# A two-block transformer forward on one core: finer places for the steps of the hybrid layers, and new orders for three engines

## The reference

```python
# first block, each of 2 layers (D_FF 2816)
f = swiglu(rms_norm(h, g1), w_gate, w_up, w_down);  h = h + 0.5 * rms_norm(f, g1_post)
u = rms_norm(h, mix_pre_g);  parts = split(u @ w_in)
y_a = short conv (3 taps);  y_b = conv (31 taps) + layer norm + silu
y_c = differential attention (4 heads);  y_d = forgetting attention (8 heads)
merged = sum(sigmoid(gate_i) * (y_i @ w_out_i));  h = h + rms_norm(merged @ w_o, mix_post_g)
f = swiglu(rms_norm(h, g2), ...);  h = h + 0.5 * rms_norm(f, g2_post)
# second block, each of 2 hybrid layers
z = rms_norm(h, g_norm) @ w_in              # 2656 columns
oa = dense GQA (q, k normed, axial rope);  ob = windowed GQA with a sink (rope)
oc = latent attention: q from a rank 192 part of z, k and v from a rank 128 part
h = h + concat(oa, ob, oc) * silu(gates) @ w_out
# at the end
return rms_norm(h, final_g)
```

## Time and profile before

| | us |
|---|---|
| median of 3 runs | 1691.02 |
| lowest, highest | 1689.95, 1692.52 |
| profiled execution, its own time | 1691.12 |
| span in its profile, first to last instruction | 1689.3 |
| TensorE busy in the span | 1646.0 |
| VectorE, ScalarE busy | 1098.7, 815.8 |

### The profile page before, as it was taken

The page is one execution under the profiler, slowest core; times in us unless marked ns, Lnnn a source line. Parts: engine busy times, 40 slices in busy tenths (PEclk is TensorE's granted clock), DMA queues, the critical chain, the costliest instruction groups (busy, mean ns, idle before and its releaser), DMA issues.

```text
span 1689.3 us, 21552 instructions
## 1 busy us (share of the span) xinstructions
PE 1646.0 (97%) x8719; PEld 1395.1 (83%) x8719; DVE 1098.7 (65%) x1314; ACT 815.8 (48%) x1116; POOL 36.5 (2%) x60
## 2 busy tenths in 40 slices
PE   8999999999999999999999999999999998999997
PEld 7888799978887888788888998788888887778776
DVE  6444668898666454655456799975665455766665
ACT  5443544454445443454445454544544446664653
POOL 0000000000000000000000000000000000000000
PEclk9999999999999999999999999999999999999999
DMA  8555465444556555565546545355555545224421
GB/s 311 196 179 199 165 219 178 162 175 150 175 174 218 181 195 182 179 216 181 194 155 224 189 168 193 126 174 195 192 206 193 181 150 162 100 93 141 135 75 50
DMA packets 67427, 292.70 MB, mean 173 GB/s; under 512 B 7152, under 2 KB 11648, under 8 KB 51456
## 3 DMA queue, kind: packets, MB, share of 16 engines
q1 hardware_dynamic: 63984, 279.47, 48.2%
q10 hardware_dynamic: 3344, 11.85, 2.0%
HBM read 290.23 MB, written 1.06 MB: 172 GB/s over the span
## 4 chain that ended last, share of the span: by engine, by line
PE 82%; DVE 9%; issue 3%; ACT 3%; DVEq 2%; DMA 1%; POOL 0%; ACTq 0%; POOLq 0%; SPq 0%
PE ps L1573 24%; PE ps L1575 24%; PE ps L1574 24%; DVE wlo L1046 3%; PE ps L2045 2%; PE ps L1736 1%; DVE mix L1243 1%; DVEq L1248 1%; PE ps L2071 1%; PE ps L1671 1%; ACT tmp L699 1%; PE ps L2056 1%; PE ps L1708 1%; PE ps L1641 1%; DVE small L1335 1%
## 5 line engine op out<-in xcount | busy, mean ns | idle before, releaser
L1046 DVE TENSOR_TENSOR wlo<-raw,whi 128x2048 fp32r<-128x2048 f32 (+2 forms) x269 | 601.2, 2243 | 259.4 <-ACT whi L696 253.9
L696 ACT ACTIVATE whi<-raw 128x2048 fp32r<-128x2048 f32 (+2 forms) x269 | 500.3, 1872 | 130.7 <-DMA raw<-stream 129.4
L1573 PE MATMUL ps<-whi,xhi 128*128 128x512 f32 (+1 forms) x1024 | 404.1, 395 | 1.1 <-ACT mix L960 1.1
L1575 PE MATMUL ps<-whi,xlo 128*128 128x512 f32 (+1 forms) x1024 | 396.2, 387 | 0.0
L1574 PE MATMUL ps<-wlo,xhi 128*128 128x512 f32 (+1 forms) x1024 | 396.2, 387 | 0.0
L1573 PE MATMUL ps<-whi,yar 128*128 128x512 f32 x620 | 245.5, 396 | 2.0 <-DVE yar L1560 1.5
L1574 PE MATMUL ps<-wlo,yar 128*128 128x512 f32 x620 | 241.0, 389 | 0.0
L1575 PE MATMUL ps<-whi,yar 128*128 128x512 f32 x620 | 241.0, 389 | 0.0
L1573 PEld LDWEIGHTS ps<-whi,xhi 128*128 128x128 f32 x1024 | 192.8, 188 | 40.7 <-issue 4.5
L1575 PEld LDWEIGHTS ps<-whi,xlo 128*128 128x128 f32 x1024 | 192.7, 188 | 39.0
L1574 PEld LDWEIGHTS ps<-wlo,xhi 128*128 128x128 f32 x1024 | 192.9, 188 | 35.3
(11 more groups left out here) (217 smaller groups left out, 1361.6 us busy)
## 6 DMA issues: line engine op xcount, KB each, us to landing
raw<-stream SPq DMA_DIRECT2D x262, 512.0 KB, 4.7
raw<-stream SPq DMA_DIRECT2D x122, 1024.0 KB, 4.8
raw<-stream SPq DMA_DIRECT2D x22, 384.0 KB, 3.9
gpre<-pre_gain ACTq DMA_DIRECT2D x8, 512.0 KB, 4.2
gpost<-post_gain ACTq DMA_DIRECT2D x6, 512.0 KB, 5.3
mix<-cum ACTq DMA_DIRECT2D x2, 1024.0 KB, 6.8
raw<-stream SPq DMA_DIRECT2D x6, 256.0 KB, 6.8
raw<-stream SPq DMA_DIRECT2D x4, 320.0 KB, 4.4
```

What stands on the lines that cost most here:

```text
L696: A(whi[:, s, 0:w], raw[:, s, 0:w], ACT.Copy).then_inc(hi_ready, 1)
L1046: TT(wlo[:, s, 0:w], raw[:, s, 0:w], whi[:, s, 0:w].bitcast(F32), ALU.subtract).then_inc(lo_v, 1)
L1573: pe.matmul(dst, lh, rh, start=first, stop=False)
L1575: return pe.matmul(dst, ll, rh, start=False, stop=last)
```

## The change

No instruction is added to or removed from the matmuls, activations or vector operations, and no tile changes its size. Four things change.

1. In the hybrid layers a half of a chunk no longer is one step but four (one k tile of a wide chunk with its 3 matmuls, two k tiles of a gate with their 6), so a chunk has eight places between which other steps of TensorE can stand. Each token half of an `out` chunk's first pass has two. Chunks of the mixing stage have two.
2. The hybrid layers' tables of all three engines have new numbers throughout.
3. In the mixing stage TensorE's `scores` 5 goes ahead of `turn` 4. On VectorE two steps of the convolution go a step earlier, the split for chunk 29 (`split` 26) goes from ahead of `scores` 5 to behind `values` 4, and `out` 2 goes behind `split` 31, `weigh` 7 and `values` 6.
4. In `boundary`, in the six that end an FFN or a mixing stage, VectorE's `low` for t = 0, second half, stands behind the two updates of `h` of t = 1, where it stood ahead of them.

The waits keep their semaphores and values; where a step became several, the wait stands at its first part. The diff, cut:

```diff
-    at(pe, (19.02, 21.02, 23.02, 25.04, 27.02, 29.02, 31.02, 33.02), "turn")
+    at(pe, (19.02, 21.02, 23.02, 25.04, 27.1998, 29.02, 31.02, 33.02), "turn")
...
     for p in range(AT_WOUT):
-        for half in range(2):
-            pe.append((p + half / 2 + 0.4, "chunk", p, half))
+        for part in range(8):
+            pe.append((p + (0.4, 0.425, 0.45, 0.475, 0.9, 0.925, 0.95, 0.975)[part], "chunk", p, part // 4, part % 4))
     for n in range(4):
-        pe.append((AT_WOUT + n / 2 + 0.4, "out", n))
-    at(pe, (3.52,), "l_turn")
-    at(pe, (6.02, 6.2376, 6.54, 6.56, 9.02, 9.04, 10.52, 10.54), "flip")
+        for part in range(2):
+            pe.append((AT_WOUT + n / 2 + 0.4 + part / 20, "out", n, part))
+    at(pe, (3.1197,), "l_turn")
+    at(pe, (5.4052, 6.1126, 6.4028, 6.4617, 8.9693, 9.1434, 10.4986, 10.6243), "flip")
...
-                        if t and not last:
+                        if t and not last and not (share and n):
                             low(X + 1, 0, n)
                     dve.drain()
                     if share:
...
                             STT(out=h[:, t, half], in0=thb[:, half], scalar=rs[:, t, 0:1], in1=h[:, t, half],
                                 op0=ALU.mult, op1=ALU.add).then_inc(h_ready, 1)
+                        if t:
+                            low(X + 1, 0, 1)
                         mean_square(q + (4 * t + 4), t, 2)
...
-            def wide_tokens(c, b, t):
+            def wide_tokens(c, b, t, ks=range(4)):
 
                 half = WIDE[c][2]
-                for k in range(4):
+                for k in ks:
                     kk = 4 * half + k
                     ins = mm3(wide_bank(b, c), xhi[:, kk, t * P:(t + 1) * P], xlo[:, kk, t * P:(t + 1) * P],
                               wide_k(whi, c, k), wide_k(wlo, c, k), kk == 0, kk == KD - 1)
+                if 3 not in ks:
+                    return
...
                         if name in Z_PAIRS:
-                            if i == 0:
+                            if i == 0 and part == 0:
                                 hyb_free(pe, l, p, half)
-                            wide_tokens(c, half, half)
+                            wide_tokens(c, half, half, (part,))
                         elif name == "gate":
-                            if half == 0:
+                            if half == 0 and part == 0:
                                 hyb_free(pe, l, p, p % 2)
-                            features(c, p % 2, (half,))
+                            features(c, p % 2, (half,), range(2 * part, 2 * part + 2))
```

More of the change, by code:

```diff
@@ L193, in mix_steps @@
     for slot, (kind, n) in enumerate(chunks):
-        pe.append((slot + 0.5, kind, n))
+        for half in range(2):
+            pe.append((slot + 0.5 + half / 20, kind, (n, half)))
     at(pe, (9.02,), "f_turn")
@@ L292, in hybrid_steps @@
[L292 to L298, removed]
@@ L299, in hybrid_steps @@
-    at(act, (6.6, 7.56, 9.08, 9.56, 10.06, 10.6, 11.36, 12.06, 12.56, 14.06), "exp")
-    at(act, (7.52, 8.52, 9.52, 10.02, 10.56, 11.32, 12.02, 12.52, 14.02, 14.52), "copy")
-    at(act, (7.58, 8.54, 9.58, 10.08, 10.92, 11.38, 12.08, 12.58, 14.08, 14.54), "o_copy")
-    at(act, (8.02,), "a_square")
-    at(act, (11.2, 11.9, 12.9, 13.9), "gate")
-    at(act, (11.369, 13.52, 15.02), "o_high")
-    at(dve, (1.52, 2.5325, 2.56, 3.54, 5.76, 7.12, 8.1, 9.06, 9.6, 10.64, 11.52, 12.6, 13.54, 14.56, 16.3), "split", range(3, 18))
@@ new lines, in hybrid_steps @@
+    at(act, (0, 0, 1.2009, 3.0722, 6.6004, 7.3136, 7.3484, 7.4213, 9.2391, 9.7951, 9.8875, 11.5645, 11.9264, 13.5379, 14.4885), "split", range(3, 18))
+    at(act, (0, 0, 4.8269, 5.2691, 5.8413, 6.4056, 6.4179, 6.4845, 7.4475, 7.5446, 9.2565, 9.5613), "take", TAKES)
+    at(act, (0.0543,), "l_square")
+    at(act, (1.5895,), "l_hi")
+    at(act, (6.4341, 6.5396, 6.7871, 7.1083, 8.5071, 8.847, 10.1345, 10.2488), "flip_copy")
+    at(act, (7.3987, 7.4945, 9.2075, 9.56, 9.721, 10.2087, 11.5264, 11.8831, 13.0461, 13.5386), "exp")
@@ new lines, in hybrid_steps @@
+    at(act, (8.1158, 8.2111, 9.52, 9.7518, 10.2672, 10.5858, 12.3594, 13.5385, 13.9937, 14.4573), "copy")
+    at(act, (8.2323, 8.2562, 9.5619, 9.8309, 10.575, 13.083, 13.5387, 13.9958, 14.4815, 14.4959), "o_copy")
+    at(act, (7.72,), "a_square")
+    at(act, (10.2831, 11.9028, 13.1649, 13.9993), "gate")
+    at(act, (12.0203, 13.991, 14.7586), "o_high")
+    at(dve, (1.9245, 1.968, 2.4196, 4.1736, 5.8115, 6.8876, 6.8982, 9.0102, 10.2115, 10.2743, 11.024, 12.0727, 13.5213, 15.1284, 15.3818), "split", range(3, 18))
@@ new lines, in hybrid_steps @@
+    at(dve, (5.7505,), "ropeg")
+    at(dve, (2.2601,), "l_norm")
+    at(dve, (2.3134,), "l_lo")
+    at(dve, (5.57,), "cq_rotate")
+    at(dve, (5.69,), "ck_rotate")
+    at(dve, (6.88, 7.3612, 9.06, 9.54, 10.1035, 10.2663, 10.8198, 11.1546, 12.1934, 12.6207), "max")
+    at(dve, (8.0675, 8.0891, 9.3, 10.103, 10.2354, 10.2817, 11.9676, 12.5579, 12.6742, 13.0818), "weigh")
+    at(dve, (8.12,), "a_mean")
+    at(dve, (8.5533, 8.7653), "a_rotate")
+    at(dve, (10.1, 10.1989), "b_rotate")
+    at(dve, (11.0498, 12.6087, 12.6601, 14.949), "gate")
@@ L1674, in turns, with rows_of @@
                         ins.then_inc(xt_done, 1)
-            def rows_of(X, ch, lh, ll, t, final, first, last=False):
+            def rows_of(X, ch, lh, ll, t, final, first, last=False, parts=(0, 1)):
                 s = ch % SLOTS
                 wh, wl = wts(whi, s, 2), wts(wlo, s, 2)
-                for a in range(2):
+                for a in parts:
                     if final and t and a and not last:
```

117 lines of the change are left out of this document (58 added, 59 removed).

## The result

The changed kernel takes 1662.04 us, the median of four executions from 1661.44 to 1664.08, against 1690.93 us for the kernel before in the same comparison: 28.9 us less, a ratio of 0.983 with a 95% interval of 0.981 to 0.985. In a second comparison it was 1661.96 to 1691.89, ratio 0.983 again. The profiled execution took 1661.44 us with a span of 1659.6, 29.7 us less than the profiled one of before.

A forecast was written before the change was run, and what follows sets the result against it. TensorE was taken to bound the kernel, busy 1646.0 of 1689.3 us. Gains of 3.5 (boundaries), 1.4 (clock), 2.4 (mixing) and 10.0 (hybrid) made 17.3 us off 1691.1: 1674.0, range 1665 to 1684.

The forecast's parts named there:

- The boundary: Six boundaries: the update of `h` starts 0.59 us earlier with `low` behind it, 3.5 us in all.
- The clock at the first entry: Entry into the first hybrid layer: with shorter, divided idle time the clock stays up, 1.4 us gained.
- The mixing stage: Two mixing stages: `scores` 5 fills the wait of `turn` 4, 1.18 us per layer, 2.4 us for both.
- the other moves on VectorE cost nothing: Mixing stage: the other moved VectorE steps delay nothing; if their cover were gone, each would cost under 1 us.
- The hybrid layers: Two hybrid layers: filled latency waits win 6.5 us, less 1.5 for returns; 5.0 us each, 10.0 in all.
- What stays: Hybrid layer: of 9.7 us of waits 3.2 stay, 1.4 at named steps and 1.8 for six thin places.
- six places with thin cover: Hybrid layer: `scores` 1, 7, 8, `turn` 3, `values` 3, first `out` given 0.3 us each, 1.8 in all.
- Returns: Hybrid layer: 13 more returns to a chunk cost 1.5 us, between a cheap 0.6 and a dear 2.9.
- rival (d): Better: 1.4 us of hybrid waits stay, returns cost 0.6, second layer's clock comes back; 23 us gained, 1668; chance 0.15.
- (a): Hybrid waits move elsewhere: 8 us gained in all, 1683; chance 0.21 including what lies between it and the forecast.
- (b): Hybrid gain is gone, the boundary chain and mixing stage gain only half: 1690.2, within 0.2%; chance 0.07.
- (c): Slower: thin float32 steps and small waits pull the hybrid layers' clock down; 1697 with 15 such stretches; chance 0.05.

The follow-up runs named there:

- The two moved splits: The changed kernel with VectorE's splits of chunks 25 and 27 put later in the mixing stage: 1658.48 us, ratio 0.9805 to the kernel before.
- the run with the places taken away: As the kernel with parts 1 and 2 alone, but attention steps can stand only between chunk halves: 1681.32 us, ratio 0.9937 to the kernel before.
- the experiment: The changed kernel with nine identity transposes added per hybrid layer, spread between gate parts (1663.90 us) or bunched behind float32 steps (1663.63).
- the kernel with the new boundary alone: The kernel before with only the boundary's `low` (t = 0, second half) moved behind the updates of `h`: 1687.48 us, ratio 0.9974.
- three of my own later edits: Latent chain moved in the kernel before (1694.59 us); on top of the two moved splits, later hybrid `scores` 3 (1665.83), then also later mixing `scores` 0 (1670.92).
- parts 1 and 2 alone: The changed kernel with the old mixing tables and the old place of `low` in the boundary: 1669.36 us, ratio 0.9868 to the kernel before.
- my four later moves: The two moved splits on the changed kernel (1658.48 us), the latent chain in the kernel before (1694.59), later `scores` 3 (1665.83), then later `scores` 0 too (1670.92).

## Why the prediction was right and wrong

**The boundary: right.** 0.59 us each was forecast by the chain, 0.61 to 0.63 came, alone and in the whole. The displaced `low` was needed, as the step said, by the second half of the low matmuls; at the sixth boundary it holds them up by 0.48 us, in the middle of the idle time, and the wait of 2.35 us became one of 0.48 and one of 0.99.

**The clock at the first entry: right.** 6.66 us became 5.30, and at this place the clock fell in five profiles of five with the old boundary and in none of eight with the new one. But behind the 2.3 us of `turn` 4 it fell in only five cases of ten: behind some 2 us of waiting it can fall in one execution and not in the next. I took the profile of before as if it were every execution of it. It had kept its clock behind `turn` 4 by luck.

**The mixing stage: half.** The swap did what it should: 2.29 us became 1.20, and `flip` 0 lost its 0.11 (in the first layer). The step that failed is "the other moves on VectorE cost nothing". I costed them one by one by who needs their result, and didn't count that two splits of 2.3 us now follow each other ahead of `o_split` 0. That is a new wait of 0.66 us, 0.82 with what isn't recorded. Wrong too was "so `turn` 4 cannot start sooner": VectorE was busy, but with a split that could wait, and moving it took away the 1.20 us that were left. The two moved splits gave back more than the new wait had cost.

**The hybrid layers: right in mechanism, less than half in size.** The term was 5.0 us a layer; the stretch gained 10.9 in the first. The mechanism, waits for latency filled by parts of chunks, is shown by the waits that left and by the run with the places taken away, in which they returned. Three sizes in the term were wrong, all in the same direction:
- *What stays.* I had 1.4 us, and added 1.8 for six places with thin cover. 0.86 us stayed: `scores` 3 with 0.56 (forecast 0.58), `scores` 2 with 0.17 (0.2), `turn` 1 with 0.14 (0.15). The reckoning was good; `l_turn` and `turn` 2, with 0.3 and 0.19 in it, do not wait at all, and none of the six thin places does. The surcharge stood for nothing in the trace. The difference is 2.3 us.
- *What a wait costs.* The sum counted recorded idle time, and so put at nothing what a wait costs beside it. Before, the stretch had 15 waits with 9.71 us recorded, but the starts behind them were 12.15 us late; after, there are three with 0.86 and 1.35. 12 waits fewer at 0.16 us are 2.0 us of gain that stood in "busy", which is why busy time fell from 105.35 to 103.27.
- *Returns.* 1.5 us were taken off; the experiment says zero. The rows had shown the late and the early start side by side, and the text even named a net of 0.1, then took 1.5, half of the dear reading of 2.9.

Together 5.0 + 2.3 + 2.0 + 1.5 = 10.8 us against 10.9 measured. The second layer gained 0.8 us more. The half clock that the prediction saw there (0.99 over the stretch) went too, but that is only part of it: by the starts it cost 1.5 us, yet the waits of `scores` 3 and `turn` 2, 0.77 us in the first layer's record, did not occur behind it. And in the kernel with the new boundary alone, whose profile shows no half clock there, the second layer is 0.7 us longer than the first all the same (111.50 against 110.79 to the end of `values` 9), with 1.64 us of waiting ahead of `l_turn` against 0.91. How the 0.8 us divide stays open. I had put the clock into rival (d) alone, with half a microsecond.

**The rivals.** (a), that waits move, came true in the mixing stage and in three of my own later edits, but not in the hybrid layers. (b) is refuted by the kernel with parts 1 and 2 alone. (c) is refuted: the profiles of the changed kernel show no half clock before its last 2 us, float32 steps spread or not, and no mean clock of it is under 0.998. (d) had the right mechanism with 1.4 us of waits staying and 0.6 for the returns, and still came out 6 us too slow: 4 of them because it too counted recorded idle time only, the rest because less stayed, the returns cost nothing and the second layer gained more. That is why the range ended too early: both of its ends were built from one biased measure.

**The rule on transposes.** The prediction named "TensorE: Matmul & The Clock Gate", section on PE-mode transpose, of the Trainium skill. Nine transposes in bunches of five and four left the mean granted clock at 0.999, as nine spread ones did, and it is 0.999 without them; so no run here shows a difference. The bunches are short, under 0.6 us each.

## What to carry to other kernels

Where an engine is bound and its waits are latency, make its work divisible and put pieces into the chain; here half of the gain needed places inside a chunk, with orders that were made for them, and an interruption cost nothing that could be measured. Price a removed wait by the distance between starts, not by the recorded idle time ahead of it. And when a step is moved, ask what it was covering: three of my four later moves only put the wait elsewhere, and in two of them it came back three times as long.

## What was not expected of the hardware

- A wait of TensorE costs 0.16 us more than the idle time recorded ahead of the next matmul (5 waits, 5.12 us recorded, 5.93 us of length), since the recorded end of the last matmul lies that far beyond its usual hold.
- Coming back from single float32 transposes to gate matmuls 18 times more cost 0.02 us, within what such stretches differ by. One transpose of 128 by 128 costs 0.105 us, recorded with 0.27.
- Behind a wait of 1.8 to 2.4 us the granted clock fell to half in some executions and places and stayed in others, with the same instructions; each time it cost 1.3 to 3.3 us. The wait of 1.2 us that is left ahead of `turn` 4 did it in no profile. Shorter waits can do it too, as in the second hybrid layer of the kernel before, behind 0.58 and 0.69 us of waiting in 2 us (windows; the clock is the third number from the end). But the same two waits in its first layer, ahead of the rows at 1454.24 and 1455.58, left the clock at 1.00. What decides it was not tried.

```profile
1596.00:1598.00 2.00, 1.31 (x8) 0.96 (x7) 1.38 (x1) 1.72 (x2) 0.00 (x0) 1.00 0.85 348
1598.00:1600.00 2.00, 2.00 (x7) 1.37 (x6) 1.09 (x3) 0.68 (x1) 0.00 (x0) 0.51 0.41 168
```
